# Attention on one Trainium2 core: exponentials issued ahead of the copies of the tile before, and the value projection of a head pair spread over two head ends

## What is computed

```
q = (_rmsnorm(q_lat, q_a_norm_w) @ w_q_b).reshape(B, L, N_HEADS, QK_DIM)
kv = (_rmsnorm(kv_lat, kv_a_norm_w) @ w_kv_b).reshape(B, L, N_HEADS, QK_NOPE + V_DIM)
k_nope, v = kv[..., :QK_NOPE], kv[..., QK_NOPE:]
...
s = jnp.einsum('bqhd,bkhd->bhqk', qi, k, preferred_element_type=F32) * scale
p = jax.nn.softmax(s, axis=-1)
return jnp.einsum('bhqk,bkhv->bqhv', p.astype(v.dtype), v)
```

## Time and profile before

| | |
|---|---|
| median of 3 runs | 1968.54 us (1963.43 to 1972.76) |
| profiled execution, time | 1966.95 us |
| profiled execution, span | 1965.2 us |
| PE busy | 1890.9 us, 96% of the span |
| DVE busy | 1023.2 us, 52% |
| ACT busy | 589.6 us, 30% |
| POOL busy | 77.3 us, 4% |
| attention loop, 80 exponentials | 64 of a prompt tile, 1212 ns each; 16 of a sample tile, 565 ns |

### The profile page before, as it was taken

How to read it: one execution, slowest core, us unless ns; L and a number is a source line. 1 busy time by engine, 2 the same in 40 slices (tenths; PEclk the granted TensorE clock), 3 DMA queues, 4 the chain that set the end, 5 groups by cost and what they waited for, 6 DMA issues and landing times.

```text
span 1965.2 us, 23786 instructions
## 1 busy us (share of the span) xinstructions
PE 1890.9 (96%) x9850; PEld 1585.8 (81%) x9850; DVE 1023.2 (52%) x1198; ACT 589.6 (30%) x837; POOL 77.3 (4%) x64
## 2 busy tenths in 40 slices
PE   8999999897999888999999999999999999999998
PEld 5666888786888777888888888888888888888887
DVE  5793677737878787665423333242433333335533
ACT  6122222426666677123202111120202111123411
POOL 0000000003122210000000000000000000000000
PEclk9999999978999999999999999999999999999999
DMA  9223253321000022410110101010111101011021
GB/s 367 74 73 110 103 194 105 107 86 66 20 20 19 15 76 89 130 43 22 43 43 33 43 32 43 32 43 32 35 40 33 42 32 43 32 69 43 22 96 54
DMA packets 36235, 127.89 MB, mean 65 GB/s; under 512 B 4363, under 2 KB 4993, under 8 KB 35652
## 3 DMA queue, kind: packets, MB, share of 16 engines
q1 hardware_dynamic: 36164, 126.91, 18.5%
HBM read 109.76 MB, written 17.13 MB: 65 GB/s over the span
## 4 chain that ended last, share of the span: by engine, by line
PE 84%; DVE 8%; ACT 3%; issue 2%; DMA 1%; POOL 1%; SPq 0%; DVEq 0%; ACTq 0%; POOLq 0%
PE ps L1980 66%; PE ps L2339 4%; PE ps L2366 2%; PE ps L2350 2%; PE ps L2039 2%; PE ps L2066 1%; PE ps L2078 1%; PE ps L2261 1%; DVE ptl L1736 1%; DVE gmax L1698 1%; DVE K L1123 1%; PE ps L2027 1%; PE ps L2126 1%; DMA wst<-wb 1%; PE ps L2273 1%
## 5 line engine op out<-in xcount | busy, mean ns | idle before, releaser
L1980 PE MATMUL ps<-XL,wh 128*128 128x512 f32 x1872 | 469.7, 359 | 0.0
L1980 PE MATMUL ps<-XH,wh 128*128 128x512 f32 (+1 forms) x1776 | 456.3, 365 | 3.8 <-DVE XL L1146 2.9
L1980 PE MATMUL ps<-XH,wl 128*128 128x512 f32 (+1 forms) x1776 | 444.8, 359 | 0.0
L1980 PEld LDWEIGHTS ps<-XL,wh 128*128 128x128 f32 x1872 | 312.9, 189 | 55.8
L1980 PEld LDWEIGHTS ps<-XH,wh 128*128 128x128 f32 x1776 | 298.8, 189 | 72.3 <-issue 18.2
L1980 PEld LDWEIGHTS ps<-XH,wl 128*128 128x128 f32 x1776 | 296.8, 189 | 53.0
L620 ACT ACTIVATE wh<-wst 128x1024 fp32r<-128x1024 f32 x98 | 103.1, 1052 | 477.5 <-PE ps L1980 470.8
L1894 DVE TENSOR_TENSOR X<-X,ps 128x1280 f32<-128x1280 f32 x64 | 95.2, 1487 | 270.2 <-PE ps L1980 270.2
L1980 PE MATMUL ps<-xhl,wh 128*128 128x512 f32 (+1 forms) x960 | 215.2, 359 | 0.0
L1884 DVE TENSOR_TENSOR dt<-dsq,dss 128x1280 f32<-128x1280 f32 x32 | 47.8, 1493 | 284.6 <-ACT dsq L987 284.4
L1980 PEld LDWEIGHTS ps<-xhl,wh 128*128 128x128 f32 x960 | 160.3, 188 | 29.0 <-issue 0.5
(11 more groups left out here) (269 smaller groups left out, 2033.1 us busy)
## 6 DMA issues: line engine op xcount, KB each, us to landing
wst<-wb SPq DMA_DIRECT2D x98, 512.0 KB, 3.2
xraw<-xT SPq DMA_DIRECT2D x8, 640.0 KB, 10.3
xt<-xt SPq DMA_DIRECT2D x10, 512.0 KB, 9.6
K<-decay SPq DMA_DIRECT2D x4, 1280.0 KB, 13.1
kf<-K SPq DMA_DIRECT2D x20, 256.0 KB, 2.4
kfr<-kf SPq DMA_DIRECT2D x10, 512.0 KB, 3.6
kscale<-kid SPq DMA_DIRECT2D x8, 640.0 KB, 4.0
X<-xT SPq DMA_DIRECT2D x8, 640.0 KB, 6.8
```

What stands on the lines that cost most here:

```text
L1980: ins = mm(acc(jslot)[:, o:o + n], sub(a[slot], s), b[:, o:o + n], start=(first and k == 0 and a is wh and b is xh), stop=(last and k == l ...
```

## The change

Two edits. First, ACT lists E(n+1) ahead of C(n) in each step instead of behind it. Second, the values of pair p are made in other steps: the first chunk in step 8 of the even head before (`t == 8`, j odd), the second and third in steps 8 and 9 of the odd head. The waits that order PSUM bank 7 are adapted. No instruction is added or dropped, and DVE's order of P and G stays.

```diff
--- before.py
+++ after.py
@@ -849,7 +849,9 @@
                     query_square(j, t)
                 if 5 <= t <= 7:
                     operand_hi(j, t - 5, True)
-                if t >= 7 and j % 2 == 0:
+                if j % 2 and j < 7 and t == 8:
+                    value_hi(j // 2 + 1, 0)
+                if t >= 8 and j % 2 == 0:
                     value_hi(j // 2, t - 7)
 
             def exponentials(n):
@@ -909,12 +911,12 @@
                 h, t, g, u = n // 10, n % 10, n // 2, n % 2
                 if g >= 2 and u == 0:
                     act.wait_ge(pv_mm, g - 1)
+                if n + 1 < 80:
+                    exponentials(n + 1)
                 for k, kt, kn in halves(n):
                     act.wait_ge(t_mm, k + 1)
                     fn(pth[g % 2][:, :].rearrange("p (k q) -> p k q", k=8)[:, kt:kt + kn, u * P:(u + 1) * P],
                        bank(4 + k % 2, kn * P).rearrange("p (k q) -> p k q", k=kn), ACT.Copy).then_inc(t_hi, 1)
-                if n + 1 < 80:
-                    exponentials(n + 1)
                 if n >= 3 and u == 1:
                     output_lo(g - 1)
                 if h < 7:
@@ -1675,7 +1677,9 @@
                     query_sums(j)
                 elif t < 7:
                     key(j, t - 4)
-                elif j % 2 == 0:
+                elif t == 8 and j % 2 and j < 7:
+                    value_lo(j // 2 + 1, 0)
+                elif t >= 8 and j % 2 == 0:
                     value_lo(j // 2, t - 7)
 
             def output(g):
@@ -2249,7 +2253,7 @@
                     weights_ready(B_ATT + j // 2 * 2)
                     if j:
                         pe.wait_ge(c_f, 6 * j)
-                        pe.wait_ge(v_lo, 3 * ((j - 1) // 2 + 1))
+                        pe.wait_ge(v_lo, 3 * ((j + 1) // 2) if j % 2 else 3 * (j // 2) + 1)
                     else:
                         pe.wait_ge(lq_lo, 2)
                         pe.wait_ge(acc_free, J_IN + 15)
@@ -2281,13 +2285,16 @@
                 if i == 0:
                     if p:
                         weights_ready(B_ATT + 2 * p - 1)
-                        pe.wait_ge(c_f, 12 * p + 3)
-                        pe.wait_ge(qs_ev, 2 * p + 1)
+                        pe.wait_ge(qs_ev, 2 * p)
                     else:
                         pe.wait_ge(wv_lo, 1)
                         pe.wait_ge(kss_ev, 1)
-                elif p or i == 2:
-                    pe.wait_ge(v_lo, 3 * p + i if p else 1)
+                elif p == 0 and i == 2:
+                    pe.wait_ge(v_lo, 1)
+                elif p and i == 1:
+                    pe.wait_ge(qs_ev, 2 * p + 1)
+                elif p:
+                    pe.wait_ge(v_lo, 3 * p + 2)
                 else:
                     pe.wait_ge(rows_ready, 2)
                 for t in range(ta, tb):
@@ -2320,7 +2327,9 @@
                     query(j, t)
                 elif t == 3:
                     query_sums(j)
-                elif t >= 7 and j % 2 == 0:
+                elif t == 8 and j % 2 and j < 7:
+                    value(j // 2 + 1, 0)
+                elif t >= 8 and j % 2 == 0:
                     value(j // 2, t - 7)
 
             def scores(n):
```

## The result

| | before | changed |
|---|---|---|
| median | 1968.56 us (4 runs) | 2000.68 us (4 runs, 1994.94 to 2003.52) |
| ratio | | 1.0154, 95% interval 1.0122 to 1.0187 |
| profiled execution, span | 1965.2 us | 1993.2 us |
| first to last exponentials | 320.8 us | 346.5 us |
| rest of the span | 1644.4 us | 1646.7 us |

The change makes the kernel 1.5% slower. The forecast was 2006, in a range of 1986 to 2022. That forecast was 39 us added to the profiled execution before; the two profiled executions differ by 28.0 us, the two medians by 32.1. Of the 28.0 us between the two profiled executions 25.7 lie between the first and the last exponentials. Two lines of the page after show what doesn't move: PE's share stays at 96%.

A forecast was written before the change was run, and what follows sets the result against it. PE, busy 292.46 of the attention loop's 323.70 us, was taken as nearly the bound. Rings, overruns and head ends summed to 361.0 against 320.8 us, 40.2 more; less about 1, +39 on 1966.95 gave 2006, range 1986 to 2022.

The forecast's parts named there:

- The ring of one step: Inside heads, each step's exponentials wait through ACT's copy and DVE's subtraction and maximum: 4.66 us against 4.06 before.
- E to C: On ACT, from the start of exponentials until the next instruction, the copy, can start: 1.32 us of each step.
- DVE's extras in step 5: DVE's other work between maximum and subtraction, 3.16 us against 1.99 of cover: 1.17 over, in odd heads 0.56.
- E(7) to E(8): Late step of each head, with a short maximum: 3.86 us plus what DVE's other work runs over.
- The ends: Six head ends, heads 0 to 5, exponentials of step 8 to the next head's second: 14.07 us, 3.1 more than before.
- the slow side: Scores and V at a head end at PE's low clock, 4.92 us, chosen over the fast row's 3.33.
- Before's ends: Head ends in the kernel before, step 8's exponentials to the next head's second: taken as 11.0 us.
- Outside the loop: After the last exponentials: about 1 us less, since the last full V no longer stands behind them.
- Steps 4.1 us apart: Sign inside heads: exponentials 4.1 us apart or less would prove the one-step ring wrong.
- a faster kernel: Rival: transposes' waits for exponentials vanish and nothing replaces them, up to 31.7 us gone: 1935 us, chance 0.06.
- The low-clock rival: PE's clock falls at six head ends, 2.6 us more at each, +15: 2021 us, chance 0.12.
- What would show it: Signs in the profile after: exponentials 4.6 to 4.7 us apart, 80 to 100 us maximum waits, PE share near 0.8.

The follow-up runs named there:

- edit 2 alone: Changed kernel with ACT's old order put back, so only the values' steps differ from the kernel before: 1968.3 us, ratio 0.9997.
- the fastest version: Kernel before with values spread, step 8's value chunk in PE's wait ahead of the next head's scores, and T(9) ahead of V: 1956.8 us, ratio 0.9943.

## Why the prediction was right

- **The size.** The time came inside the range and 5 us from the forecast, but part of that is luck. The loop was to lose 40.2 us and lost 25.7; the medians, 32.1 us apart, lie nearer to the forecast than the profiled executions on which it was built.
- **The ring of one step.** Right in kind, place and sign. 4.66 was forecast, 4.52 and 4.57 came. The term that was off is E to C: 1.32 us, read from an output copy behind an exponential; C itself starts 1.19 us behind (602.96 to 604.15). The profile before had rows for this: 30 copies `oc` of 64 partitions start 1.31 to 1.34 us after a prompt tile's exponentials, 14 other instructions, such as the copies `qh`, `kh` and `wh`, 1.18 to 1.20. The other links came as read: 0.62, 1.21, 1.46, and 0.04 to 0.09. Over 48 rings that is 5.1 us. The ring was weighed against 4.06 us, the mean of all 79 steps with the short ones of the sample tiles; inside the heads the step was 4.27, so the margin was smaller than the text had it.
- **The two edits.** The forecast split the loss by place: 3.1 us more at each of six ends, the rest in the rings. Against the real loop before, its rows say 20.2 us for E(1) to E(8) and 20.2 for the six ends; 9.7 and 15.8 came. Alone, edit 1 costs 20 us (1.0103) and edit 2 nothing (0.9997), though together they cost 32: with edit 1 in both, edit 2 makes the ends 9.6 us longer in the sum (80.0 against 70.4) and leaves the steps as they are. In edit 2 alone the ends grow by 7.7 us and the steps give 7.9 back. That the ring is what keeps them from giving it back is my reading; no run isolates it.
- **DVE's extras in step 5.** Forecast 1.17 and 0.56 us over the cover, came 0.47 and nothing. That is 4.2 us too much over the heads; the other 1.1 by which the row "E(7) to E(8)" is off are E to C again. The key product that I had read took 1.46 us in the profile before, while POOL's `kl` product ran; after, it took 0.69, begun 0.30 us behind the end of `kl`. DVE, then POOL, in step 5 of head 2, before:

```profile
560.60 1.46 DVE L1657 TENSOR_TENSOR wst<-zc,kscale 64x512 f32<-64x512 f32 x1
```

```profile
560.22 1.29 POOL L1061 TENSOR_TENSOR kl<-wst,kh 128x512 fp32r<-128x512 f32 x1 [6.94 <-ACT kh L829]
```

and after:

```profile
573.28 0.69 DVE L1659 TENSOR_TENSOR wst<-zc,kscale 64x512 f32<-64x512 f32 x1
```

```profile
571.71 1.27 POOL L1063 TENSOR_TENSOR kl<-wst,kh 128x512 fp32r<-128x512 f32 x1 [5.07 <-ACT kh L829]
```

  The row was no outlier: six of the seven products of step 5 took 1.31 to 1.46 us before. What the forecast missed is that the new order pulls POOL and DVE apart there.
- **The ends.** 14.07 forecast, 13.5 to 13.7 at five and 12.1 at one. The pieces came as read (S(10) at 3.29, forecast 3.40; S and V 4.90, forecast 4.92); E to C, twice, was 0.24 too long in all, the value copy 0.1. Head 2's end ran at the full clock, 3.38 us for S and V (580.49 to 583.87) where the fast row had 3.33. Five of six took the slow side, in part by luck. The reason given was that PE's idle time ahead of S(10) grows, and it did; but head 2's end had the same waits as head 3's (1.55 us ahead of T(8) and 0.87 ahead of S(10), against 1.57 and 0.86). So these waits alone don't decide the level, and what does stays open. The sentence of the Trainium skill ("TensorE: Matmul & The Clock Gate", section "Loop structure matters more than you think") that was weighed there speaks of products that follow at once; at these ends they don't, so it decides neither way.
- **Before's ends.** The text took 11.0 us for each; head 0's was 9.4 and head 6's 11.8. Head 0's did not enter the sum, which goes by the whole loop; head 6's did, as 11.0 "as now", and 11.3 came.
- **Outside the loop** 1 us less was forecast, 2.3 more came; that is inside what this part varies by.
- **Rivals.** Steps 4.1 us apart, and a faster kernel, needed a ring shorter than PE's work; the rows of DVE and ACT excluded that. The low-clock rival was right that the clock falls further (0.93), but it gave no time beyond the forecast: five of the ends had the low level in their sum, and the step with low stretches in it (E(5) to E(6) in heads 1 to 6) is still 4.51 or 4.52 us.
- **What would show it.** Even steps, waits for the maximum (88.0 us with those under "issue", 80 to 100 forecast), P 0.62 us behind C, the value copy's six waits and the end of the copies' waits for transposes (62.9 us to 2.9) came. PE's busy share came at 0.88, not 0.8: the loop was 14 us shorter than the sum, and PE's own busy time grew by 14 us, since products at the low clock count as busy for longer.

## What to carry to other kernels

Before moving an instruction ahead on one engine, write down the rings: from the instruction through every engine and back to its next instance, and count how many steps each ring spans. A ring that goes through two engines' list order and spans one step sets a floor on the step however idle the engines are; moving one block can turn a two-step ring into a one-step ring, and the gaps it was meant to close come back on the engine that was moved. Where a copy gates the next stage, ask what the product that it copies stands behind on its engine: taking T(9) from behind V, with the value chunk already in the gap, made the kernel 0.6% faster than it was before (0.9943), which moving the exponentials did not. On the kernel before the same move alone gained nothing that the times show.

## What the runs showed of the hardware

- Stretches of low granted clock move, and their number changes, when the order of work changes. In the loop there were 9 before, 14 in the changed kernel, 6 with edit 2 alone and 5 in the fastest version, at mean granted clocks of 0.95, 0.93, 0.97 and 0.97. The scores of step 4 took 1.05 us a pair in five heads before and the full-clock 0.62 with edit 2 alone, whose products in that step are the same; the ends got low stretches instead. What decides where a stretch falls stays open.
- DVE's key product of 64x512 (`zc` by `kscale`) took 1.31 to 1.46 us the six times that POOL's `kl` product was running when it began (profile before), and 0.67 to 0.69 us the 22 times that none did (profiles before and after).
- The next instruction on ACT after exponentials of 128x1024, where it had nothing to wait for, started 1.31 to 1.34 us after their start when it was a copy of 64 partitions from PSUM, and 1.18 to 1.20 when it was a copy of 128 partitions, from PSUM or not.
- The span outside the loop varied from 1641 to 1655 us between single profiled executions of kernels with the same code there. Times of single executions can't tell differences under some 10 us of this kernel; the ring's steps, 4.52 and 4.57 us in turn, repeat to 0.02 us in three kernels, head 0 aside.
